# Where ScalarE's feature steps stand in the order of an RWKV recurrence

## The reference

```python
def wkv7_scan(s0, r, w, kk, a, k, v):
    def step(s, inp):
        r_t, w_t, kk_t, a_t, k_t, v_t = inp
        s_kk = jnp.einsum('bhvk,bhk->bhv', s, kk_t)
        s = (s * w_t[:, :, None, :] - s_kk[..., None] * (kk_t * a_t)[:, :, None, :]
             + v_t[..., None] * k_t[:, :, None, :])
        return s, jnp.einsum('bhvk,bhk->bhv', s, r_t)
```

## Time and profile before

| | us |
|---|---|
| median of three runs | 3087.43 |
| lowest and highest | 3086.93, 3090.69 |
| the profiled execution | 3085.09 |
| its span, first to last instruction | 3083.5 |

### The profile page before, as it was taken

How to read it: one execution, slowest core, us unless ns; L and a number is a source line. 1 busy time by engine, 2 the same in 40 slices (tenths; PEclk the granted TensorE clock), 3 DMA queues, 4 the chain that set the end, 5 groups by cost and what they waited for, 6 DMA issues and landing times. The chain is left out here.

```text
span 3083.5 us, 62817 instructions
## 1 busy us (share of the span) xinstructions
PE 2859.8 (93%) x26751; PEld 2331.1 (76%) x26751; DVE 1897.7 (62%) x3016; ACT 1428.7 (46%) x2197; POOL 526.2 (17%) x482
## 2 busy tenths in 40 slices
PE   7899899998899889999889999999989977999999
PEld 2795677777778658887549999999956744678877
DVE  4941565555665257765778888888864256466652
ACT  1212555655554242221347777777734345343231
POOL 1001545545542010000010000000010045100000
PEclk9999999999999999999999999999989988999999
DMA  5553000000000277655249999999922210222222
GB/s 206 193 191 127 23 21 21 21 21 21 3 3 4 82 255 277 267 198 199 87 153 424 367 369 363 369 367 372 366 99 105 87 36 19 89 77 96 96 96 82
DMA packets 73843, 482.11 MB, mean 156 GB/s; under 512 B 11107, under 2 KB 13027, under 8 KB 32144
## 3 DMA queue, kind: packets, MB, share of 16 engines
q1 hardware_dynamic: 59360, 418.48, 36.0%
q0 software_dynamic: 11952, 51.91, 4.6%
q10 hardware_dynamic: 2304, 8.39, 0.7%
HBM read 457.20 MB, written 34.13 MB: 159 GB/s over the span
## 5 line engine op out<-in xcount | busy, mean ns | idle before, releaser
L2360 DVE TENSOR_TENSOR sb_moe_w_lo<-w_ring,sb_moe_w_hi 128x1408 fp32r<-128x1408 f32 (+1 forms) x132 | 255.3, 1934 | 69.9 <-ACT sb_moe_w_hi L2305 68.3
L2208 PE MATMUL ps<-sb_moe_w_hi,sb_x_feat_lo 128*128 128x352 f32 x832 | 273.4, 329 | 5.2 <-DVE sb_moe_w_lo L2360 5.1
L2210 PE MATMUL ps<-sb_moe_w_hi,sb_x_feat_hi 128*128 128x352 f32 x832 | 267.5, 321 | 0.0
L2209 PE MATMUL ps<-sb_moe_w_lo,sb_x_feat_hi 128*128 128x352 f32 x832 | 266.8, 321 | 0.0
L2305 ACT ACTIVATE sb_moe_w_hi<-w_ring 128x2816 fp32r<-128x2816 f32 x80 | 204.3, 2554 | 2.5 <-DMA w_ring<-w_moe_up 1.8
L2208 PE MATMUL ps<-sb_moe_w_hi,sb_hid_feat_lo 128*128 128x256 f32 x572 | 163.2, 285 | 3.9 <-DVE sb_hid_feat_lo L2491 3.9
L2208 PEld LDWEIGHTS ps<-sb_moe_w_hi,sb_x_feat_lo 128*128 128x128 f32 x832 | 156.1, 188 | 11.5 <-issue 10.4
L2210 PE MATMUL ps<-sb_moe_w_hi,sb_hid_feat_hi 128*128 128x256 f32 x572 | 161.8, 283 | 0.0
L2209 PE MATMUL ps<-sb_moe_w_lo,sb_hid_feat_hi 128*128 128x256 f32 x572 | 161.8, 283 | 0.0
L2209 PEld LDWEIGHTS ps<-sb_moe_w_lo,sb_x_feat_hi 128*128 128x128 f32 x832 | 157.0, 189 | 0.0
L2210 PEld LDWEIGHTS ps<-sb_moe_w_hi,sb_x_feat_hi 128*128 128x128 f32 x832 | 156.0, 187 | 0.0
(11 more groups left out here) (540 smaller groups left out, 7751.2 us busy)
## 6 DMA issues: line engine op xcount, KB each, us to landing
w_ring<-w_moe_up SPq DMA_DIRECT2D x67, 1408.0 KB, 8.4
sb_hm<-w_ada SPq DMA_DIRECT2D x48, 1024.0 KB, 7.1
w_ring<-w_ffn SPq DMA_DIRECT2D x22, 1024.0 KB, 4.9
w_ring<-w_up SPq DMA_DIRECT2D x22, 1024.0 KB, 4.8
sb_b_again<-w_moe_up SPq DMA_DIRECT2D x13, 1408.0 KB, 8.6
sb_hm<-w_moe_up SPq DMA_DIRECT2D x13, 1408.0 KB, 8.2
sb_t_again<-w_moe_up SPq DMA_DIRECT2D x13, 1408.0 KB, 7.7
w_ring<-w_moe_down SPq DMA_DIRECT2D x13, 1408.0 KB, 7.3
```

The costliest lines, as they stand in the source:

```text
L2208: pe.matmul(out, x_lo, w_hi, start=first, stop=False)
L2209: pe.matmul(out, x_hi, w_lo, start=False, stop=False)
L2210: return pe.matmul(out, x_hi, w_hi, start=False, stop=end)
L2360: return V.tensor_tensor(WL[:, s, w], raw[raw_at(c, i)[0]][:, w], WH[:, s, w].bitcast(F32), ALU.subtract)
```

## The change

While an index is in `quiet`, a feature or output step that is GpSimd's is not put in, and with the change one that is ScalarE's is not either. It waits until the next index outside `quiet` (162, 165 or 171 here), where all that is due by then goes in together. A pair of steps that the planner keeps together (a `w` or `a` matmul with ScalarE's copy of it) is exempt, as before.

```diff
@@ -1026,7 +1026,7 @@
                     due = len(side) * min(max(i - lo, 0), hi - lo) // (hi - lo)
                     if at and done[0] < len(early):
                         continue
-                    while done[at] < len(side) and (done[at] < due and (side[done[at]][2][0] != "G" or i not in quiet)
+                    while done[at] < len(side) and (done[at] < due and (side[done[at]][2][0] not in "GA" or i not in quiet)
                                                     or done[at] and side[done[at]][2] in ("Aw0", "Aw1", "Aa0", "Aa1")
                                                     and side[done[at] - 1][2] == "P" + side[done[at]][2][1:]):
                         plan.append(side[done[at]])
```

## The result

The changed kernel takes 3121.24 us (median of four runs, 3110.68 to 3124.6) against 3089.06 us (3086.93 to 3090.98), a ratio of 1.0103 with a 95% interval of 1.0087 to 1.0119. It is slower by 32 us, where I forecast 24, and outside my range. The stall came nearly as computed (3.24 us a pair instead of 3.1). What hung on it by way of the clock was more than twice what I took.

A forecast was written before the change was run, and what follows sets the result against it. PE, the fullest engine in the pairs, was taken to bound them, with ScalarE mattering where PE waits for it. Stall 18.6 plus clock 5.1 gave 23.7 us, forecast 3111 us against 3087.4, range 3100 to 3117.

The forecast's parts named there:

- The stall: Pairs 1 to 6: Y4 on PE starts 3.1 us later behind U4's late copy, 18.6 us in all.
- the clock: Pairs 1 to 6: PE's new idle time lowers the granted clock, 0 to 1.7 us each, 0.85 taken, 5.1 in all.
- The path to W4's and U4's copies: ScalarE, pairs 1 to 6: W4's copy behind load and three exponentials, U4's behind Pi1 too, making U4's copy 3.1 us later.
- No gain from the earlier copies: T4 copies without Px0 ahead could release score8 earlier, 0 to 0.3 us a pair; 0 taken.
- Nothing gives it back: Behind Y4 and on GpSimd, nothing stays in place to absorb the 3.1 us a pair.
- The table load: ScalarE: the load goes with Px0 onto the path, 1.29 us a pair, without the skill's 1.38 us of drain.
- GpSimd's gap ahead of kdk: Sign in the changed profile: this wait would be about 3.1 us instead of 2.6.
- my middle: Clock cost of 0.85 us for each of six places, between bounds of 0 and 1.7.
- The sum: Whole kernel: 18.6 us of stall plus 5.1 of clock, 23.7 us, forecast 3111.
- The range's high end: Clock at its bound, 18.6 + 10.2 = 28.8 us, 3116, and one for the spread of runs.
- Rival 1: Pairs 1 to 6: the stall without the clock, 18.6 us, 3106; chance 0.18.
- Rivals 2 to 4: Delay partly absorbed at later sums, 11 us, 3098, chance 0.10; faster, 3081, 0.03; gain and loss cancel, 3087, 0.04.

The follow-up runs named there:

- e6: Changed kernel plus two 128x512 constant matmuls on PE ahead of its wait for W4's copy, one ahead of U4's, in pairs 1 to 6: 3106.9 us, ratio 1.0058.
- e8: Kernel before the change, with the exponential Pi1 alone moved behind trans10's copies: 3094.5 us, ratio 1.0019.
- e4: Changed kernel with W4's copy moved ahead of the three exponentials Px0, Pi0 and Px1: 3117.4 us, ratio 1.0093.
- e3: Changed kernel with a one-column Exp behind U3's copy in pairs 1 to 6, drawing the table load to an idle place: 3101.0 us, ratio 1.0036.
- e1_again: The changed kernel run again with no edit, for a second trace and more times: 3118.8 us, ratio 1.0093.
- e5: Changed kernel with the five exponentials and the table load behind U4's copy: 3096.9 us, ratio 1.0030.

## Why the prediction was right and wrong

- **The path to W4's and U4's copies: right.** I had 3.50 us of load and exponentials ahead of W4's copy, one more exponential ahead of U4's, and 3.1 us at Y4. Measured from score8 to Y4: 3.24. Two small terms were off and partly cancel: the exponential right ahead of W4's or U4's copy takes 0.85 and 0.87 us from start to start, not 0.73, and trans8's copies start 0.12 us earlier behind score8. With the clock held up (e6) the six stalls make 18.5 to 19.6 us, against my 18.6.
- **No gain from the earlier copies: right.** From T4.4 to score8 are 1.24 us in pair 3 before (634.57 to 635.81) and 1.23 after (646.83 to 648.06), so taking Px0 from in front of the T4 copies gave score8 nothing.
- **Nothing gives it back: right.** The waits on GpSimd's and VectorE's sums are the same, e8 shows that even 0.73 us a pair comes through, and e4 that kka's time is of no weight. GpSimd's gap ahead of kdk is 3.1 us on average in e6, as forecast, and 4.6 in the trace after, where the clock makes kd1 later still.
- **The table load: right.** It cost 1.29 us a pair on the path (e3). Px0 starts 1.29 us behind the load's start in the trace after, as in the earlier trace rows, and the load 0.02 behind the end of the copies before it. The further 1.38 us of drain that the Trainium skill gives ("ScalarE: Activation LUTs", section "What ACT_TABLE_LOAD costs") does not show there either.
- **The clock: the step that failed.** I had set "3.4 / 2 = 1.7 us" as the upper bound of what a fall costs and took 0.85 a pair, 5.1 us. It cost 11.0 us in the first trace and 12.6 in the second, 1.8 to 2.1 a pair, above the bound. The mechanism was named. What was wrong was the length: I took the single fall of the earlier trace rows for the longest there can be. Of the twelve falls in two traces, the three that lasted 3.4 us cost 0.5 each, less than my middle. The nine that lasted 6.8 cost 2.1 to 2.7 each. The part of a fall ahead of Y4 is free, and the rest costs close to half its length: in pair 2, 6.8 - 1.8 = 5.0 us, of which 2.3 are lost.
- The trace before had the warning. Just behind the stage that I read, the clock was low for 10.2 us (from 1013.8 to 1024 us), with PE idle 1.72 us ahead of line 1309 and 1.44 ahead of line 1313:

```profile
1012.00:1014.00 2.00, 0.82 (x24) 0.68 (x24) 0.00 (x0) 0.28 (x1) 0.78 (x1) 0.92 0.15 33
1014.00:1016.00 2.00, 1.46 (x2) 0.50 (x2) 0.00 (x0) 0.00 (x0) 0.48 (x1) 0.50 0.99 319
...
1022.00:1024.00 2.00, 2.00 (x3) 0.67 (x2) 2.00 (x3) 0.00 (x0) 0.00 (x0) 0.52 0.00 0
```

- **The sum.** With the stage's 30.1 instead of 23.7 it is 3087.4 + 30.1 = 3117.5, 4 below the first median and 1 below e1_again's. Of those 4 us 1.6 are the median before, which came out at 3089.1 in this comparison. The range's high end, 3117, had the clock at its bound, so both medians lie above it.
- **Rivals.** Rival 1, no fall of the clock, is what e6 makes by hand. Rivals 2 to 4 fell with the first trace.

What stays open is why a fall lasts 3.4 us in one pair and 6.8 in another. The two traces of the same kernel have the short ones in different pairs (3 and 6, and 4). They are the three of the twelve that began earliest, 2.2 to 2.3 us ahead of Y4, and the other nine began 0.8 to 2.1 ahead. No run tests whether that decides it, and e4's two short ones began behind Y4. Why the convolution stage was 4.5 us shorter in one execution is not shown either.

## What to carry to other kernels

Work of a side engine that fills its waits is free where it is, and costs nearly its full length just behind them, ahead of a copy that a chain reads (3.24 us a pair here for the 3.5 of load and exponentials ahead of W4's copy and Pi1 ahead of U4's). Before holding such work out of a phase, list what stands right behind the phase on the same engine: here the release point was the chain's own steps, and e5 shows that even two steps later it is not free. Where a change makes TensorE idle for some microseconds, price the lower clock as a term of its own, with the longest stretch known as no more than a lower bound of the longest possible.

## What the runs showed of the hardware

- The granted clock fell to its lower level behind 2.6 us of idle time, 0.3 to 1.8 us after narrow matmuls had started again, in all of twelve places of two traces, and stayed there for 3.4 or 6.8 us. Behind two waits of up to 1.3 us in the same place (e3) it fell in one of six, and behind single waits of 1.5 us (e5) and 1.6 us (e8) in none.
- A fall of 6.8 us cost 2.1 to 2.7 us of time and one of 3.4 us 0.5, where its first part lay ahead of a wait for ScalarE. The one fall of e3 began just behind Y4, lasted 3.4 us and cost 1.5 (from Y4 to the next long matmul 5.42 us instead of 3.88).
- Three matmuls of constants in those waits (e6) kept it at 2.4 GHz and took some 11 us off the stage, though they compute nothing.
- An fp32 matmul of 128x512 is two instructions and takes 0.87 us at the higher level; the count in a timeline row is of instructions.
- On ScalarE, exponentials of 128x768 that follow each other start 0.73 to 0.75 us apart, though each is recorded with 0.82 to 0.84 us. The copies of W4 and U4 start 0.85 and 0.87 us behind the exponential ahead of them.
